# A one-layer streaming encoder block in fp32: opening chunk reordered, norm sums in two short matmuls, weight loads issued in front of the stores

## The reference

```python
u = rms_norm(h, g_pre_mix); z = u @ w_in            # 1024 x 3840
z_glu, q, k, v, z_gate = split(z)
a, b = split(z_glu); c = a * sigmoid(b)
c = silu(layer_norm(causal_depthwise_conv(c, 31 taps)));  y_conv = c @ w_conv_out
y_attn = sliding_window_sink_attention(rope(q), rope(k), v, sinks) @ w_attn_out
y = sigmoid(gA) * y_conv + sigmoid(gB) * y_attn
h = h + rms_norm(y @ w_out, g_post_mix)
gate, val = split(rms_norm(h, g_pre_ffn) @ w_up)     # 1024 x 5632
f = (gelu(causal_depthwise_conv(gate, 3 taps)) * val) @ w_down
h = h + rms_norm(f, g_post_ffn)
h = h + (p @ w_ple) * sigmoid(h @ w_ple_gate)
```

## Time and profile before

| | |
|---|---|
| median of 3 runs | 2790.68 us |
| profiled execution: its time | 2789.94 us |
| its span, first to last instruction | 2788.1 us |
| mean granted TensorE clock | 0.998 |
| TensorE (PE) busy | 2745.9 us, 98% |
| VectorE (DVE) / ScalarE (ACT) / GpSimd (POOL) busy | 1385.1 / 761.8 / 520.8 us |
| DMA | 606.8 MB, mean 218 GB/s |

### The profile page before, as it was taken

How to read it: one execution, slowest core, us unless ns; L and a number is a source line. 1 busy time by engine, 2 the same in 40 slices (tenths; PEclk the granted TensorE clock), 3 DMA queues, 4 the chain that set the end, 5 groups by cost and what they waited for, 6 DMA issues and landing times.

```text
span 2788.1 us, 31297 instructions
## 1 busy us (share of the span) xinstructions
PE 2745.9 (98%) x12292; PEld 2250.2 (81%) x12292; DVE 1385.1 (50%) x2262; ACT 761.8 (27%) x1371; POOL 520.8 (19%) x614
## 2 busy tenths in 40 slices
PE   6999999999999999999999999999999999999999
PEld 5887788888788888888888888888888888888887
DVE  8786677644632376653343245766335312613234
ACT  2423321212443142121245223211115512311012
POOL 5667377776430000000000000000000000000000
PEclk9999999999999999999999999999999999999999
DMA  6777688777675555555555655555555555555554
GB/s 227 269 250 270 250 289 291 291 284 276 233 270 209 214 191 201 192 196 194 185 195 197 240 195 183 207 196 192 186 196 188 198 214 193 198 190 193 196 195 168
DMA packets 169059, 606.79 MB, mean 218 GB/s; under 512 B 18768, under 2 KB 19024, under 8 KB 168912
## 3 DMA queue, kind: packets, MB, share of 16 engines
q1 hardware_dynamic: 164304, 596.39, 58.8%
q10 hardware_dynamic: 4608, 8.39, 0.8%
HBM read 468.39 MB, written 136.31 MB: 217 GB/s over the span
## 4 chain that ended last, share of the span: by engine, by line
PE 93%; DVE 2%; DMA 2%; POOL 1%; ACT 1%; issue 0%; SPq 0%; DVEq 0%
PE ps L792 26%; PE ps L793 25%; PE ps L794 25%; PE ps L816 5%; PE ps L817 5%; PE ps L820 5%; DMA w_stage<-in_weights 2%; POOL w_lo L437 1%; PE ps L872 1%; PE ps L900 1%; PE ps L828 1%; PE ps L890 0%; POOL w_hi L434 0%; DVE ssum L1191 0%; DVE y_lo L1524 0%
## 5 line engine op out<-in xcount | busy, mean ns | idle before, releaser
L792 PE MATMUL ps<-y_hi,w_hi 128*128 128x512 f32 x1536 | 601.7, 392 | 2.2 <-POOL w_lo L437 2.2
L793 PE MATMUL ps<-y_lo,w_hi 128*128 128x512 f32 x1536 | 598.4, 390 | 0.0
L794 PE MATMUL ps<-y_hi,w_lo 128*128 128x512 f32 x1536 | 598.3, 390 | 0.0
L437 POOL TENSOR_TENSOR w_lo<-w_stage,w_hi 128x256 fp32r<-128x256 f32 x488 | 386.4, 822 | 9.8
L792 PEld LDWEIGHTS ps<-y_hi,w_hi 128*128 128x128 f32 x1536 | 288.6, 188 | 64.6 <-issue 4.9
L793 PEld LDWEIGHTS ps<-y_lo,w_hi 128*128 128x128 f32 x1536 | 288.7, 188 | 61.6 <-issue 1.9
L794 PEld LDWEIGHTS ps<-y_hi,w_lo 128*128 128x128 f32 x1536 | 288.7, 188 | 60.3
L1259 DVE SCALAR_TENSOR_TENSOR ps<-conv_in,col,ps 128x512 f32<-128x512 f32 x452 | 309.9, 746 | 0.0
L792 PE MATMUL ps<-f_hi,w_hi 128*128 128x512 f32 x768 | 302.0, 393 | 2.9 <-ACT ple_first L629 2.7
L794 PE MATMUL ps<-f_hi,w_lo 128*128 128x512 f32 x768 | 299.4, 390 | 0.0
L793 PE MATMUL ps<-f_lo,w_hi 128*128 128x512 f32 x768 | 299.4, 390 | 0.0
(11 more groups left out here) (172 smaller groups left out, 3670.6 us busy)
## 6 DMA issues: line engine op xcount, KB each, us to landing
w_hi<-split_weights SPq DMA_DIRECT2D x366, 512.0 KB, 3.2
w_lo<-split_weights SPq DMA_DIRECT2D x366, 512.0 KB, 4.2
w_stage<-in_weights SPq DMA_DIRECT2D x122, 512.0 KB, 3.7
split_weights<-w_hi SPq DMA_DIRECT2D x122, 512.0 KB, 2.9
split_weights<-w_lo SPq DMA_DIRECT2D x122, 512.0 KB, 3.9
x_in<-in_x SPq DMA_DIRECT2D x16, 512.0 KB, 5.7
h<-in_x SPq DMA_DIRECT2D x16, 512.0 KB, 5.7
out_h<-h ACTq DMA_DIRECT2D x32, 256.0 KB, 2.5
```

The source lines that it names most:

```text
L437: last = nc.gpsimd.tensor_tensor(w_lo[:, slot, k:k + 2], w_stage[:, slot, k:k + 2], w_hi[:, slot, k:k + 2].bitcast(F32), ALU.subtract)
L792: nc.tensor.matmul(bank, w_hi[:, slot, kk], hi, start=start, stop=False)
L793: nc.tensor.matmul(bank, w_hi[:, slot, kk], lo, start=False, stop=False)
L794: return nc.tensor.matmul(bank, w_lo[:, slot, kk], hi, start=False, stop=stop)
```

## The change

It is one diff of several edits. Line numbers of the new kernel differ.

1. **SP's loop.** `load_block(n)` now stands in front of `store_block(n-2)`. `load_block` and its two waits stay as they were.
2. **Fresh blocks on TensorE.** `full_block`, `by_tile`, `conv_outs`, the first chunk's `attention_outs` and the down projections with eight tiles wait only for the rounded part (`rounded_there`), issue the 16 products that need it, then wait for the remainder and issue the other eight.
3. **Short norm sums.** For 14 of the 20 sums ScalarE rounds `ssum` into `s_hi` (`sum_round`), VectorE subtracts into `s_lo` (`sum_rest`), and TensorE multiplies both by an fp32r matrix of ones: two fp32r matmuls in place of one fp32 matmul. Of these, 4 fall into the opening chunk and 10 behind it.
4. **Opening.** TensorE runs three fp32 matmuls on zeros before the first norm and four behind it (`warm_up`). The first norm's eight squares are summed by eight fp32 matmuls into the bank, not by VectorE. ScalarE loads the root's table at the start (`warm_root`). VectorE computes most of the angles ahead of the first norm. The positions are loaded ahead of the input, the identity matrix behind the third weight block.
5. **Moved steps.** `value_rows(0)` moves into the first gate block, the sum for chunk 1's input ahead of the last tiles of the `w_out` block group, and ScalarE's `h3_tile(c, 7)` behind the evictions `ple_evict(c, 4)` to `(c, 7)`.

```diff
@@ block.sync
-            for t in range(TT):
-                load_x(0, t)
             load_positions(0)
+            for t in range(TT):
+                load_x(0, t)
             for n in range(len(ORDER)):
                 c, b = ORDER[n]
-                if n >= SLOTS - 1 and FRESH[n - (SLOTS - 1)]:
-                    store_block(n - (SLOTS - 1))
...
                 load_block(n)
+                if n == SLOTS - 1:
+                    sp.dma_start(ident[:, :], identity).then_inc(ident_loaded, 16)
+                if n >= SLOTS - 1 and FRESH[n - (SLOTS - 1)]:
+                    store_block(n - (SLOTS - 1))
@@ block.tensor
             def full_block(c, b, bank, hi, lo, between=None):
+                if FRESH[PLACE[c, b]]:
+                    rounded_there(c, b)
+                    for k in range(8):
+                        if k == 4 and between is not None:
+                            between()
+                        by_rounded(ps[:, bank], c, b, k, hi[:, k], lo[:, k], k == 0)
+                    ready(c, b)
+                    for k in range(8):
+                        last = by_remainder(ps[:, bank], c, b, k, hi[:, k], k == 7)
+                    last.then_inc(block_done, 1)
+                    return
                 ready(c, b)
...
             def token_sums(kind, c):
+                if summed_in_parts((kind, c)):
+                    pe.wait_ge(ones_rounded, 1)
+                    pe.wait_ge(s_hi_ready, PART_AT[kind, c] + 1)
+                    nc.tensor.matmul(bank, ones_r[:, :], s_hi[:, :], start=True, stop=False)
+                    pe.wait_ge(s_lo_ready, PART_AT[kind, c] + 1)
+                    nc.tensor.matmul(bank, ones_r[:, :], s_lo[:, :], start=False, stop=True).then_inc(ssum_done, 1)
...
-            token_sums(X, 0)
+            warm_up(3)
+            for j in range(KD_):
+                pe.wait_ge(sq_ready, SQ_AT[X, 0] + j + 1)
+                sums = nc.tensor.matmul(ps[:, XS], ones[:, :], sq[:, j % 2], start=j == 0, stop=j == KD_ - 1)
+                sums.then_inc(ss_added if j < KD_ - 1 else ssum_done, 1)
+            warm_up(4)
@@ block.vector
-            x_norm(0)
+            zero_sum()
+            angle_start(0)
+            angle_turns(0)
+            angle_rest(0)
+            angle_turns(1)
+            token_norm(X, 0, D)
...
-            angles(0)
             glu(0, 0)
+            angle_rest(1)
             glu(0, 1)
```

More of the change, by code:

```diff
@@ L803, in full_block, with next_input_sums, by_tile @@
                 last.then_inc(block_done, 1)
-            def by_tile(c, b, banks, hi, lo, hi_there, lo_there, count, between=None):
+            def next_input_sums(c):
+                pe.wait_ge(merged, c * KD_ + KD_)
+                token_sums(X, c + 1)
+            def by_tile(c, b, banks, hi, lo, hi_there, lo_there, count, between=None, last_part=None):
                 n = len(banks)
+                if FRESH[PLACE[c, b]]:
+                    for i in range(n):
+                        if 2 * i == n and between is not None:
+                            between()
+                        if i == n - 1 and last_part is not None:
+                            last_part()
+                        ks = range(i * 8 // n, (i + 1) * 8 // n)
+                        rounded_there(c, b + i)
+                        for k in ks:
+                            first = k * n % 8
+                            slot = PLACE[c, b + i] % SLOTS
+                            pe.wait_ge(hi_there, count + k + 1)
+                            for o in range(n):
+                                nc.tensor.matmul(ps[:, banks[o]], w_hi[:, slot, first + o], hi[:, k], start=(k == 0), stop=False)
+                            pe.wait_ge(lo_there, count + k + 1)
+                            for o in range(n):
+                                nc.tensor.matmul(ps[:, banks[o]], w_hi[:, slot, first + o], lo[:, k], start=False, stop=False)
+                        ready(c, b + i)
+                        for k in ks:
+                            for o in range(n):
+                                last = by_remainder(ps[:, banks[o]], c, b + i, k * n % 8 + o, hi[:, k], k == 7)
+                        last.then_inc(block_done, 1)
+                    return
                 for k in range(8):
@@ L909, in gate_b_block, with first_attention_outs @@
                 full_block(c, GB_BLOCK[j], GB_BANK[j % 2], u_hi, u_lo, between=between)
+            def first_attention_outs(i, b):
+                rounded_there(0, b)
+                pe.wait_ge(ao_lo, SUB)
+                if i == 0:
+                    pe.wait_ge(conv_tap, sum(CONV_RUN[j][-2][0] + 1 for j in (2, 3)) + 2 * TAPS)
+                for n in range(2):
+                    if i:
+                        pe.wait_ge(merged, 2 * i + n - 1)
+                    for k in range(NC):
+                        by_rounded(ps[:, AT_BANK[n]], 0, b, NC * n + k, ca_hi[:, NC + k], ca_lo[:, NC + k], k == 0)
+                ready(0, b)
+                for n in range(2):
+                    for k in range(NC):
+                        last = by_remainder(ps[:, AT_BANK[n]], 0, b, NC * n + k, ca_hi[:, NC + k], k == NC - 1)
+                last.then_inc(block_done, 1)
             def attention_outs(c, i):
                 b = AT_BLOCK[i]
+                if c == 0:
+                    first_attention_outs(i, b)
+                    return
                 ready(c, b)
                 pe.wait_ge(ao_lo, c * SUB + SUB)
-                if i == 0 and c == 0:
-                    pe.wait_ge(conv_tap, sum(CONV_RUN[j][-2][0] + 1 for j in (2, 3)) + 2 * TAPS)
                 for n in range(2):
@@ L1003, in down @@
                         between()
+                    if c == 0 and count == 8:
+                        full_block(c, B_DN[q] + j, dn_bank(q, j), f_hi, f_lo)
+                        continue
                     for k in range(count):
```

132 lines of the change are left out of this document (95 added, 37 removed).

## The result

| | before | after |
|---|---|---|
| median of the runs made together (four each) | 2790.05 us | 2889.50 us |
| lowest to highest | 2788.75 to 2790.76 us | 2887.97 to 2889.69 us |
| span of the profiled execution | 2788.1 us | 2887.9 us |

The ratio is 1.0353, with a 95% interval of 1.0337 to 1.0369: the changed kernel is 3.5% slower, as forecast. The forecast was 2899 us, 9.5 us too high, and the range of 2858 to 2938 holds the result.

What follows compares the result with a forecast made beforehand. TensorE, busy 2745.9 of 2788.1 us, was taken as the bound. 2789.94 + 114 (lateness from the load-store ring) - 4.5 (ten short norm sums) = 2899.4, rounded to 2899 us; range 2858 to 2938.

Steps and rivals of the forecast that it cites:

- The ring: SP's queue: load n, two stores, landing, load n+1; 6.69 to 7.04 us against TensorE's 5.44 us per block.
- the ring doesn't bind: Rival: last store lands within 5.44 us of the load, TensorE keeps its pace; 27 us gained, 2763 us; chance 0.04.
- a ring of 5.6 to 5.7 us: Rival: some 100 rings lose 0.2 us each, about eating the 27 us gain; 2788 us; chance 0.03.
- I take 6.85: Ring length in us chosen between the commonest and the mean of eight groups; ends 6.69 (sum 2883) and 7.04 (2918).
- the second leg: SP's loads for uses 55 to 113: 58 x 6.85 = 397.3 us, and 2.5 for `p_feat` and positions.
- Load 3: Opening: this load goes out at about 31.0 us, before at 31.97; the faster opening passes on only about 1 us.
- Load 45: Opening chunk: goes out at 327.4 us, after 42 rings of 6.85 (287.7) and five tiles at 1.73 (8.7).
- Block 45: End of opening chunk on TensorE: ends at 339.0 us, before 309.19; 30 us late, which stay over the reloads.
- Block 113: Ends on TensorE at 789.6 us, before at 683.23: 106 us late.
- The last leg: Uses 114 to 136: 22.4 us for sixteen fresh blocks, less about 10 and 2.7; 8 added, 114 us late.
- What would show it: Profile signs: fresh loads every 6.7 to 7.0 us, SP's landing waits over 500, TensorE's weight waits over 90, DMA about 230 GB/s.
- The clock rival: Rival: TensorE's clock falls in every block from its waits, at most 0.3 us each; about 2930 us; chance 0.08.

Runs made afterwards that it cites:

- a longer and a shorter ring: Changed kernel with a third 512 KB store per fresh block: 3046.31 us; changed kernel, remainder's store first, fresh loads waiting for it alone: 2792.43 us.
- the base: The changed kernel with SP's loop in the old order (store of block n-2, then load n), everything else kept: 2772.06 us, ratio 0.9929.

## Why the prediction was right, and where its terms were off

**The ring.** The step on which all rests, that moving the load ahead of the store closes a ring that is longer than TensorE's pace, is shown: by the order put back (5.44 us, -117 us), by the order alone (+118 us on before), and by a longer and a shorter ring. The rival "the ring doesn't bind" falls, and so does the one of a ring of 5.6 to 5.7 us. By the Trainium skill, "DMA: Bandwidth & Descriptors", section "Anatomy of one DMA", I had an estimate of 5.6 us for 1.57 MB; the traces have 6.63 in the median of 113, and no single one under 5.97. I had not said what that section's fit is for: one DMA, issued from GpSimd. Here SP issues three, so the estimate carried it further than it is stated. The same section of the Trainium skill says that a transfer's semaphore counts only once its last byte is confirmed in the target memory, and that this lasts longest for HBM. It would fit a load that lands in 4.1 us and two stores behind it in 5.0 and 5.7, but these run side by side, so no run here separates the confirmation from the queueing.

**"I take 6.85".** This term was mis-sized. I had weighed in the slow groups among eight. The ring measured 6.69 from load to load in the median, my own low end, and 6.64 in the mean of the second leg, (759.51 - 374.62)/58. I had also argued that late landings are not made good; there were only five of them in 113. By my own low end the sum was 2883; the result lies between.

**The legs,** by SP's timeline of after (the loads for uses 3, 45, 55, 113 and 141):

```profile
32.65 0.33 SPq L397 DMA_DIRECT2D w_stage<-in_weights  x1
...
316.26 0.33 SPq L397 DMA_DIRECT2D w_stage<-in_weights  x1
...
374.62 0.33 SPq L397 DMA_DIRECT2D w_stage<-in_weights  x1
...
759.51 0.33 SPq L397 DMA_DIRECT2D w_stage<-in_weights  x1
...
933.76 0.32 SPq L399 DMA_DIRECT2D w_hi<-split_weights  x1
```

- *Load 3* was put at 31.0 and went out at 32.65. "Only about 1 us gets through" was too much for this execution: block 0 ended at 32.6, and before at 31.9. The clock fell at 27.5 us, in the middle of block 0 (see the last section). With the same opening and the order put back it fell at 22.2, and load 3 went out at 31.09, 0.9 us ahead of before, so the size of this term depends on where that fall lies.
- *Load 45* was put at 327.4 and went out at 316.26. From load 3 these are 283.6 us where I had 296.4: 4.2 of the 12.8 are 42 shorter rings (6.75 here, with most of the late ones), the other 8.6 are the tiles of `x` and `h`, **the step that was plainly wrong**. I gave each tile 1.73 us of the ring, and it costs about 0.1. It is issued *behind* the two stores, while SP would wait for them anyway, and lands behind them:

```profile
249.46 0.33 SPq L397 DMA_DIRECT2D w_stage<-in_weights  x1
...
250.78 1.38 SPq L381 DMA_DIRECT2D x_in<-in_x  x1
256.27 0.33 SPq L397 DMA_DIRECT2D w_stage<-in_weights  x1
```

  Such a ring took 6.81 us; the next three 6.74, 6.73 and 6.68. The third store of the experiment, of the same size and in the same place, cost 1.3 us: there the load waited for it.
- *Block 45* ended 20 us late (forecast 30), at 329.3, 13.0 us behind its load where I had 11.6. "The 30 us stay" over the reloads did not hold: load 55 went out 25.5 us late. The 5.5 us more are three waits of TensorE between 329 and 375 us: 1.5 for ScalarE's tile of chunk 1's input, 2.5 for a reloaded remainder, and 1.5 for which the profile shows no releaser.
- *Block 113* ended at 770.0 (768.13, and 8 x 0.227), 87 us late where I had 106: 15 of the 19 us come from the second leg (12.4 from shorter rings, 2.5 from `p_feat` and the positions, which cost nothing that can be seen), the rest is what was left of the first.
- *The last leg* was mis-sized the other way. I added 8 us and it was 17: the load for use 141 went out at 933.76, before at 829.58 (not among the rows of before), 104.2 us late. Where a two-part reload goes out with the stores of a fresh block behind it, the ring holds four transfers in place of three, which my sum had not counted; it had the loads *gain* some 10 us of lead on these reloads:

```profile
765.73 0.32 SPq L399 DMA_DIRECT2D w_hi<-split_weights  x1
...
773.95 0.33 SPq L397 DMA_DIRECT2D w_stage<-in_weights  x1
```

  That step is 8.22 us, and later ones of this kind, at 808.90 and 817.42, take 8.52 and 10.21. TensorE's waits of 9.0 and 5.1 us at L818 lie in this leg.

**The sum.** 104.2 - 10 x 0.45 = 99.7, and the spans differ by 2887.9 - 2788.1 = 99.8. In this pair of profiles the term for the ten short sums came out to 0.1 us. Against the forecast of 109.5 that is 9.8 too little: the rings -16.6, tiles and positions -11.1, load 3 +1.7, the end of block 45 +1.4, the reloads in a row +5.4, the last leg +9.8, and -0.3 for block 113. So errors of 28 us one way met errors of 18 the other way. That the forecast was only 9.5 us off is in part luck: the number was better than its parts.

**What the rest is worth.** For the case without a ring I had 27 us; it is 19. Of these, 6 to 7 are the short sums (I had 6.3), 4 to 5 the rounded part first (7.2), 3 the filler matmuls. SP's loads show where most of the remainder lies: between the loads for uses 126 and 130 the base wins 4.5 us on before. There before has the wait of 2.7 us for ScalarE and a fall of the clock behind it, and the base has neither. Which of the moved steps took them away was not tried; nor was the 3.0 us wait at the second GLU pair, which is gone from the earlier trace rows in the base. Of the clock's 5 us about 3.4 came: before has three falls, at 244.5, 302.5 and 759.9 us, each worth 1.7, and the base has one, at 22.2. Base and after both have this fall in the opening, where TensorE runs ahead of VectorE's scaling. In the window of 27.0 to 31.5 us of after the granted clock was 0.62:

```profile
27.00:31.50 4.50, 3.92 (x10) 3.15 (x11) 4.47 (x7) 1.32 (x3) 1.11 (x1) 0.62 0.00 0
```

**What would show it.** Right: SP's wait (642 us), loads every 6.7 us, DMA at 237 GB/s, chunks 1 to 3 shorter by 4.4 us (99.8 against 104.2 at the load for use 141). Too large: TensorE's waits for rounded weights, 61.7 us in 69 places for "over 90 in some 90", mean 0.9 for 1.2 to 1.5, partly because of the 0.25 us booked as busy. Wrong: "none in the attention part" (five, 3.5 us, between 100 and 200 us), and "busy time as before, less some 6 us", which rose by 35. The clock rival falls: with waits of about 0.9 us in each block the mean of the four runs lay between 0.996 and 0.998.

## What to carry to other kernels

Where a buffer is refilled by the same queue that empties it, write down the loop: which transfer each load waits for, and how many issues lie between that transfer and the load. With the store one issue earlier its landing is hidden behind a whole block; directly behind a load it is a ring, whose length (issue, landing, wake-up) is to be compared with the time in which the consumer uses a buffer up, and the surplus is paid per block. In a profile such a ring looks as if nothing were the limit: every engine and the DMA below what they reach without it, the consumer's waits small and spread, and one large wait on the issuing queue. Here, transfers that went out in the ring's wait and that no load waited for cost about 0.1 us each, and taking the landing of just one transfer out of the wait gave 97 of 117 us back.

## What the runs showed of the hardware

- **In the opening of after the clock fell behind several short waits.** TensorE waited 1.82, 0.82, 0.25, 1.07 and 0.88 us between 19.4 and 27.6 us, none of them as long as the 2 us in the earlier trace rows that I had read as the mark, and the clock fell at 27.5. Nor does one longer wait decide it: in before, the wait of 3.0 us, which ends at 51.3 us, left the granted clock at 1.00 from 51 to 60 us. So the length of a single wait was too simple a reading. The last row of these five in TensorE's timeline, where the slower pairs (1.22 us for two, elsewhere 0.6 to 0.7) set in:

```profile
27.58 1.22 PE L877 MATMUL ps<-u_lo,w_hi 128*128 128x512 f32 x2 [0.88 <-DVE u_lo L1339]
```

- **With longer waits in each block it fell again and again.** The kernel with the third store, whose waits were mostly 2.0 to 2.5 us, had 38 falls, and a granted clock of 0.93 from 420 to 680 us; after, with 0.9 us, had 1.00 there. Even so the time followed the ring (1.29 us for each fresh block): the slower products took time that TensorE would otherwise have waited.
- **Landings have a tail.** The same three transfers land within 0.1 us of 6.64 in about 73 of 113 places, and up to 8.2 at times; how often differed between two kernels that issue them alike (5 of 113 at 7.15 us or more, and 14 of 113). The cause stays open. It sets how far a ring's cost can be forecast, here 11 us.
